# DeltaNet's triangular inverse: levels 1 to 4 on diagonal blocks of 32 rows, and the four chunks written out

## The reference

```python
gamma = jnp.exp(jnp.where(tril, gc[..., :, None] - gc[..., None, :], -jnp.inf))
kb = k * beta[..., None]
low = jnp.where(strict, jnp.einsum('bhncd,bhnsd->bhncs', kb, k) * gamma, 0.0)
rhs = jnp.concatenate([v * beta[..., None], kb * jnp.exp(gc)[..., None]], axis=-1)
sol = lax.linalg.triangular_solve(jnp.eye(c, dtype=low.dtype) + low, rhs,
                                  left_side=True, lower=True)
u, w = sol[..., :dv], sol[..., dv:]
def step(s, xs):
    u_c, w_c, attn_c, qd_c, kd_c, gl_c = xs
    v_new = u_c - jnp.einsum('bhcd,bhde->bhce', w_c, s)
    o = jnp.einsum('bhcd,bhde->bhce', qd_c, s) + jnp.einsum('bhcs,bhse->bhce', attn_c, v_new)
    s = s * jnp.exp(gl_c)[..., None, None] + jnp.einsum('bhcd,bhce->bhde', kd_c, v_new)
    return s, o
```

## Time and profile before

| | us |
|---|---|
| median of 3 runs | 1856.23 |
| lowest and highest | 1850.76, 1856.71 |
| the profiled execution, its own time | 1854.68 |
| span of the profiled execution | 1853.0 |
| one prompt chunk (four of them) | 50.3 to 50.5 |
| the sample chunk, up to its first memory product | 14.4 |

### The profile page before, as it was taken

The page is one execution under the profiler, slowest core; times in us unless marked ns, Lnnn a source line. Parts: engine busy times, 40 slices in busy tenths (PEclk is TensorE's granted clock), DMA queues, the critical chain, the costliest instruction groups (busy, mean ns, idle before and its releaser), DMA issues. The chain is left out here.

```text
span 1853.0 us, 36268 instructions
## 1 busy us (share of the span) xinstructions
PE 1760.0 (95%) x13404; PEld 1636.5 (88%) x13404; DVE 1012.1 (55%) x1848; ACT 722.0 (39%) x1239; POOL 403.2 (22%) x580
## 2 busy tenths in 40 slices
PE   8999899999799999999999999799899999999997
PEld 6999788888598999999999998555598999999997
DVE  4763455551528766767225433576537666678224
ACT  4343333331536333335224311556446333336222
POOL 1554344453001222221000000343300222221000
PEclk9999999998899999999999999899999999999999
DMA  4222211100521222223222224889721222222322
GB/s 174 79 79 80 71 35 35 34 20 1 193 80 57 87 83 79 79 85 102 91 91 69 80 68 156 290 290 326 256 84 54 84 85 79 79 82 75 101 90 86
DMA packets 78367, 188.61 MB, mean 102 GB/s; under 512 B 9442, under 2 KB 25186, under 8 KB 77906
## 3 DMA queue, kind: packets, MB, share of 16 engines
q1 hardware_dynamic: 71618, 168.47, 26.8%
q0 software_dynamic: 6672, 19.10, 3.1%
HBM read 176.00 MB, written 11.55 MB: 101 GB/s over the span
## 5 line engine op out<-in xcount | busy, mean ns | idle before, releaser
L674 PE MATMUL PB<-parts,wparts 128*128 128x288 f32 x8664 | 1170.2, 297 | 21.9 <-DVE wparts L643 10.9
L674 PEld LDWEIGHTS PB<-parts,wparts 128*128 128x128 f32 x8664 | 1164.6, 190 | 26.1 <-DVE wparts L643 21.1
L633 ACT ACTIVATE wparts<-ring 128x1024 fp32r<-128x1024 f32 x198 | 209.8, 1059 | 684.8 <-PE PB L674 683.9
L643 DVE TENSOR_TENSOR wparts<-ring,wparts 128x1024 fp32r<-128x1024 f32 x174 | 212.8, 1224 | 274.3 <-ACT wparts L633 264.7
L1033 POOL COPY cnew<-arena 128x2 f32 (+1 forms) x106 | 115.1, 1085 | 344.0 <-DVE arena L958 341.2
L970 DVE SCALAR_TENSOR_TENSOR arena<-arena,ffw 128x512 f32<-128x512 f32 x176 | 133.7, 760 | 19.4 <-DVE arena L971 12.8
L955 DVE TENSOR_TENSOR arena<-PB,stats 128x288 f32<-128x288 f32 x88 | 40.2, 457 | 127.8 <-PE PB L674 121.2
L684 PE MATMUL PB<-parts,wparts 128*128 128x288 f32 x648 | 104.7, 310 | 3.9 <-DVE parts L513 3.3
L684 PEld LDWEIGHTS PB<-parts,wparts 128*128 128x128 f32 x648 | 91.0, 188 | 12.9 <-DVE parts L513 7.3
L1009 DVE SCALAR_TENSOR_TENSOR arena<-arena,dnw 128x512 f32<-128x512 f32 x54 | 58.0, 1075 | 32.8 <-ACT arena L908 27.6
L932 ACT ACTIVATE arena<-arena,ffw 128x512 f32<-128x512 f32 x88 | 63.8, 725 | 27.0 <-issue 15.5
(11 more groups left out here) (299 smaller groups left out, 2091.8 us busy)
## 6 DMA issues: line engine op xcount, KB each, us to landing
ring<-in_w SPq DMA_DIRECT2D x198, 512.0 KB, 3.2
arena<-in_kpages SPq DMA_DIRECT2D x64, 256.0 KB, 5.5
arena<-in_vpages SPq DMA_DIRECT2D x64, 256.0 KB, 5.2
arena<-in_kpages POOLq DMA_DIRECT2D x64, 128.0 KB, 2.8
arena<-in_vpages POOLq DMA_DIRECT2D x64, 128.0 KB, 5.0
membuf<-in_w SPq DMA_DIRECT2D x8, 512.0 KB, 5.7
arena<-in_state_dn SPq DMA_DIRECT2D x6, 512.0 KB, 5.0
o_dns_s<-arena SPq DMA_DIRECT2D x6, 512.0 KB, 3.9
```

The lines of the kernel that those rows point to most:

```text
L633: nc.scalar.activation(wparts[:, 0, k, :], ring[:, k, :], ACT.Copy).then_inc(hi_ready, 1)
L643: nc.vector.tensor_tensor(wparts[:, 1, k, :], ring[:, k, :], wparts[:, 0, k, :].bitcast(F32), ALU.subtract).then_inc(lo_ready, 1)
L674: last = nc.tensor.matmul(dst(b), wparts[:, part, k, block * P:(block + 1) * P], x[:, row_, b * HALF:(b + 1) * HALF], start=start and part ...
```

## The change

Levels 1 to 4 only join blocks inside the diagonal blocks of 32 rows. The changed kernel keeps for them only those blocks: four blocks of 32 x 32 for a head and chunk, stored as 128 partitions by 32 columns, so that a group of three heads has 96 columns where it had 384. `LTb`, `BTb`, `TXb` (Tm and TT side by side) and `M1b` are these compact tiles. `blocks` issues each product as four products of 32 x 32 x 32: each has its operands on partitions 32i to 32i+31 and writes to PSUM partitions 32i to 32i+31, that is to its own row and column tile of the array. All of a group's results lie in one PSUM bank. One subtraction of 192 columns then serves Tm and TT of a group.

At the start, `lc` forms the compact lower matrix from the four diagonal blocks, `tt0` makes TT in two small steps and Tm by VectorE's own transposition in blocks of 32, so `t0` and its copy on ScalarE fall away. The full `lb` is formed after level 1, and `vt` (the turning of v on TensorE) moves behind level 1 and waits for it. After level 4, `full` spreads the blocks to 128 x 128 (`em` to Tm, `et` to TT, each times the mask `block4`). Levels 5 and 6 are as before, with `kd` behind level 5. GpSimd forms the masks of levels 2 to 4 in one step. The sample chunk, of 64 positions and levels 1 and 2, uses the same steps with two blocks. Finally the loop over chunks is written out, so no register is computed in it.

```diff
-            for step, g in ((kk, 0), (kq, 0), (kk, 1), (kt, 0), (kt, 1), (kq, 1), (vt, 0), (t0, 0), (vt, 1), (t0, 1)):
+            def blocks(out, left, right):
                 for h in range(3):
+                    for i in range(T // 32):
+                        b = slice(32 * i, 32 * i + 32)
+                        last = nc.tensor.matmul(out[b, h, :], left[b, h, :], right[b, h, :], start=True, stop=True)
+                return last
+            for step, g in ((kk, 0), (kq, 0), (kk, 1), (kt, 0), (kt, 1), (kq, 1)):
                 step(g)
             for l in range(1, levels):
+                if l <= 4:
+                    for g in G:
+                        wait("pool", f"bt{min(l, 2)}_{g}")
+                        wait("dve", f"tt0{g}" if l == 1 else f"x{l - 1}_{g}")
+                        blocks(bank_b(2 * g, T), BTb[0:T, g, l - 1, :, :], TXb[g][0:T, 0, :, :]).then_inc(S_, mark(f"m{l}_{g}"))
+                    for g in G:
+                        wait("act", f"m{l}_{g}")
+                        if l == 1:
+                            wait("dve", f"at{g}")
+                        if l < levels - 1:
+                            blocks(bank_b(2 * g + 1, T), TXb[g][0:T, 1, :, :], M1b[g][0:T, 0, :, :])
+                        blocks(bank_b(2 * g + 1, T, 1), M1b[g][0:T, 0, :, :], TXb[g][0:T, 1, :, :]).then_inc(S_, mark(f"x{l}_{g}"))
+                    if l == 1:
+                        vt(0)
+                        vt(1)
+                    continue
...
+            def lc(g):
                 wait("pe", f"bb{g}")
                 wait("dve", f"lt{g}")
+                for i in range(T // 32):
+                    b = slice(32 * i, 32 * i + 32)
+                    last = nc.vector.tensor_tensor(LTb[b, 3 * g:3 * g + 3, :], heads(LT, g, T, T)[b, :, b],
+                                                   bank(4 + g, T, T)[b, :, b], ALU.mult)
+                last.then_inc(S_, mark(f"lc{g}"))
...
-            for step, g in ((kn_, 0), (qn_, 0), (kn_, 1), (lt, 0), (lb, 0), (qn_, 1), (lt, 1), (lb, 1), (tt0, 0), (tt0, 1),
-                            (vb_, 0), (at, 0), (vb_, 1), (at, 1)):
+            for step, g in ((kn_, 0), (qn_, 0), (kn_, 1), (lt, 0), (lc, 0), (qn_, 1), (lt, 1), (lc, 1), (tt0, 0), (tt0, 1),
+                            (at, 0), (at, 1)):
                 step(g)
             for l in range(1, levels):
                 for g in G:
+                    if l <= 4:
...
+                        nc.vector.tensor_tensor(tx, tx, PB[0:T, 2 * g + 1, 96 * x0:192].rearrange("p (x h n) -> p x h n", x=2 - x0, h=3),
+                                                ALU.subtract).then_inc(S_, mark(f"x{l}_{g}"))
+                        continue
...
+                elif l == 1:
+                    lb(0)
+                    lb(1)
+                elif l == 2:
+                    vb_(0)
+                    vb_(1)
+                elif l == 4:
+                    for g in G:
+                        full("em", Tm, 0, g)
+                        full("et", TT, 1, g)
+                elif l == 5:
+                    kd(0)
+                    kd(1)
...
-            with eng.Fori(0, NCH // 2) as i:
+            for i in range(NCH // 2):
```

More of the change, by code:

```diff
@@ L56 @@
 LEVELS_S = 3
+DN_CONST = 8 * P + 6 * 32
 class Steps:
@@ L314, in heads, with heads_b, bank_b @@
             return a[0:rows, 3 * g:3 * g + 3, 0:T]
+        def heads_b(a, g, T=P):
+            return a[0:T, 3 * g:3 * g + 3, :]
+        def bank_b(b, T=P, x=0):
+            return PB[0:T, b, 96 * x:96 * x + 96].rearrange("p (h n) -> p h n", h=3)
         def bank(b, rows=P, T=P):
@@ L341, in dn_table @@
             act += "os0 os1 ol0 ol1 or0 or1"
-            dve = "ga00 ga01 ga02 ga10 ga11 ga12 kn0 qn0 kn1 lt0 lb0 qn1 lt1 lb1 tt00 tt01 vb0 at0 vb1 at1 "
+            dve = "ga00 ga01 ga02 ga10 ga11 ga12 kn0 qn0 kn1 lt0 lc0 qn1 lt1 lc1 tt00 tt01 at0 at1 "
             for l in range(1, n):
                 for g in G:
-                    if l < n - 1:
+                    if l <= 4:
                         dve += f"x{l}_{g} "
-                    dve += f"xt{l}_{g} "
-                if l <= 2:
-                    dve += f"kd{l - 1} wk{l - 1} "
+                    else:
+                        dve += f"x{l}_{g} xt{l}_{g} " if l < n - 1 else f"xt{l}_{g} "
+                if sample:
+                    dve += f"vb{l - 1} kd{l - 1} wk{l - 1} "
+                else:
+                    dve += {1: "lb0 lb1 ", 2: "vb0 vb1 ", 4: "em0 et0 em1 et1 ", 5: "kd0 wk0 kd1 wk1 "}.get(l, "")
+            if sample:
+                dve += "et0 et1 "
             if sample:
@@ L353, in dn_table @@
                 dve += "s0 s1 s2 s3 s4 s5 on0 on1 oz0 oz1"
-            pool = "ug ib vst bt0_0 bt0_1 bt1_0 bt1_1 " + " ".join(f"bt{l}" for l in range(2, n)) + " qd"
+            pool = "ug ib vst bt1_0 bt1_1 bt2_0 bt2_1 " + ("" if sample else "bt5 bt6 ") + "qd"
             if sample:
@@ L1240, in dn_pe @@
                     for h in range(3 * g, 3 * g + 3):
-                        last = nc.tensor.matmul(bank(g, T, T)[:, h - 3 * g, :], BT[0:T, h, 0:T], Tm[0:T, h, 0:T],
+                        last = nc.tensor.matmul(bank(2 * g, T, T)[:, h - 3 * g, :], BT[0:T, h, 0:T], Tm[0:T, h, 0:T],
                                                 start=True, stop=True)
@@ L1256, in dn_pe @@
             for g in G:
-                wait("dve", f"xt{levels - 1}_{g}")
+                wait("dve", f"et{g}" if sample else f"xt{levels - 1}_{g}")
                 wait("dve", f"wk{g}")
@@ new lines, in full @@
+            def full(name, dst, x, g):
+                wait("dve", f"x{4 if not sample else levels - 1}_{g}")
+                n = T // 32
+                nc.vector.tensor_tensor(heads(dst, g, T, T).rearrange("p h (j n) -> p h j n", j=n),
+                                        TXb[g][0:T, x, :, :].unsqueeze(2).to_broadcast([T, 3, n, 32]),
+                                        block4[0:T, 0:T].rearrange("p (j n) -> p j n", j=n).unsqueeze(1).to_broadcast([T, 3, n, 32]),
+                                        ALU.mult).then_inc(S_, mark(f"{name}{g}"))
```

122 lines of the change are left out of this document (73 added, 49 removed).

## The result

The changed kernel takes 1878.75 us (median; 1873.64 to 1881.13) where the kernel before takes 1855.39 in the same comparison: a ratio of 1.012, with an interval of 1.0097 to 1.0144. It is 1.2% slower. The forecast was 1835 us, 1% faster, with a range up to 1863: wrong in its sign, and outside its range.

The account below looks back on a forecast made before the run. TensorE's own work was taken to bound levels 1 to 4. Gains of 1.5 + 7.6 - 1.15 = 7.9 us a chunk, less 2.9 for the clock, leave 5.0, 20 for four chunks: 1835 us, range 1821 to 1863.

Parts of the forecast that it names:

- the written-out loop at zero: Loop over chunks: second chunk (new code) 50.39 us, fourth 50.48, so new code and looping cost nothing.
- the supply is the wall: Small-product levels: instructions come no faster than 15 ns each, 4.4 us a level; 1863 us, chance 0.15.
- the clock: Levels 1 to 5: TensorE's granted clock falls under small tiles and waits, costing 2.9 us a chunk, ends 0 and 4.5.
- The middling supply: Small-product levels: an instruction every 8.5 ns, 2.45 us a level; 1843 us, chance 0.20.
- Level 1: Second chunk up to m2: m1 and m2 start earlier, a gain of 1.5 us a chunk.
- The sample chunk: Sample chunk, two levels: lost turning and copy balance the added lc, et, vb and kd steps; zero within 1 us.
- the line of the columns: VectorE step time by column count, from 384 and 192 columns: 96 columns take 0.17 us, lc's four steps 0.68.
- Tiles that take turns: Small products: four tiles writing one PSUM bank wait for each other, 4.3 us a level; 1863 or 1915 us, chance 0.08.
- the sign that the prediction named against turns: Changed profile: with turns, matmuls of different tiles would start evenly spaced, and not four together.
- the length of the levels where code is kept: Levels 2 to 4: 1.74 us each in place of 4.26 at full clock, 7.6 us saved a chunk.
- the end of the inverse: Levels 5 and 6: return to full size loses 1.15 us a chunk at full clock; kd is covered by level 6.
- the prediction's estimate: TensorE's instruction issue: about 20 cycles at a 1.2 GHz sequencer clock, 16.7 ns each, 4.8 us a level.

Follow-up runs that it names:

- the first run: The kernel before with only its loop over the four chunks written out, old inverse kept: 1857.62 us, ratio 1.0006.
- the third run: The changed kernel with TensorE's code for one chunk in a loop of two rounds inside a loop of two rounds: 1861.31 us, ratio 1.0029.
- the sixth run: The changed kernel with levels 2 to 4 of a prompt chunk as a three-round loop in TensorE's code, chunks written out: 1859.47 us, ratio 1.0022.
- the ninth run: The kernel with levels 2 to 4 looped, chunks written out, plus dense products that nothing reads where TensorE waits: 1858.62 us, ratio 1.0026.
- the eighth run: The kernel with 64-row blocks, plus v's turning moved, em of both groups ahead of et, GpSimd's scaling later: 1838.17 us, ratio 0.9912.
- the seventh run: The changed kernel's scheme with 64-row blocks in levels 1 to 5, masks behind the first waiting for tt0: 1851.16 us, ratio 0.9977.
- the fifth run: The changed kernel with GpSimd's masks of levels 2 to 4 waiting for tt0 of the second group: 1868.0 us, ratio 1.0063.

## Why the prediction was wrong, by its steps

**The step that failed: the written-out loop at zero.** The prediction read from the earlier trace rows that the second chunk, in new code, takes as long as the fourth, and concluded that "neither new code nor looping costs anything at that rate". The rows were read rightly: the first run shows the same. But the rate belongs to the old inverse, 72 instructions in a level of 4.26 us; the change asks for 288 in 1.74, ten times the rate, and this step was not asked again at the new one. In levels 2 to 4 of the second chunk 864 loads and matmuls took 12.98 us, 15.0 ns each; kept code did the same in 8.27 (9.6 ns) at a clock of 0.57. This is 4.7 us a chunk at most, and 2.3 in the fourth (10.6 us). Over the four chunks the three levels took 12.8, 13.0, 12.1 and 10.6 us where 8.2 were forecast: 15.7 of the 38.6 us between the forecast and the profiled execution (1873.64). It is the largest step and not the only one: without it the third and sixth runs stand at 1861 and 1859, still not faster than before, because of the steps below.

**The rival "the supply is the wall"** had the price, 15 ns an instruction, right by accident: it came from a run bound by its columns. Its mechanism was wrong, since kept code is no slower than 6.1 ns (below), so a loop could cure it, and its 1863 us left out what else failed. It was also set up as an alternative to the clock and to the other losses. All came together, and the range's upper end should have been their sum. The middling supply put one rate, 8.5 ns, on all code, where the runs show two, for new code and for kept; and its gain of 5.3 us a chunk would make some 1833.5 us, so the 1840 to 1845 given for it does not lie between its own two sums.

**The clock**: right in kind. It fell in level 1 and came back for good in levels 5 and 6 (0.60, 0.63, 0.70). Its price of 2.9 us a chunk, with ends of 0 and 4.5, fits what the runs show: the ninth run's fourth chunk, at full clock, is 2.3 us shorter than the sixth's, 1.0 us in level 1 and 1.6 in levels 5 and 6, and holds six fillers of 0.22 to 0.49 us in its levels 2 to 4 besides. By an estimate from these rows the price is then some 3.6 us, from 2.3 with fillers that cost nothing to 5.

**Level 1** was to gain 1.5 us up to m2 and lost 1.2 (17.96 us from the chunk's start instead of 16.80). Of the 2.6 us between that and the forecast, m1 came 1.1 later than worked out, 0.8 of it by the two lc: each took 1.08 us to the next step where 0.68 had been read off the line of the columns:

```profile
272.59 1.04 DVE L1467 TENSOR_TENSOR arena<-arena,PB 32x96 f32<-32x96 f32 x4
273.67 0.26 DVE L1478 TENSOR_TENSOR arena<-arena,pconst 128x96 f32<-128x96 f32 x1
```

Then the tt0 of the second group lost 0.8 beside GpSimd, where 0.4 had been added; and the turning of v, with level 2 queued behind it, took 1.51 us at the lower clock, where three products of 0.11 had been counted. The eighth run, with the turning behind level 2 among its four moves, takes 44.5 us for the chunk where the seventh takes 47.1.

**The sample chunk** was put at zero within 1 us, and lost 6.2. What was missed is a cover that was none: the prediction saw the GpSimd steps beside tt0 in the prompt chunks, and did not ask what GpSimd does in the sample chunk at that place. It was the scaling of q (1.00 us) and a piece of the weight scaling (1.89 us). The fifth run gave back 3.8 of the 6.2 us; no run shows what the other 2.4 are.

**Tiles that take turns** (0.08): not so. One group's m in the second chunk, 24 matmuls in four tiles of one bank:

```profile
274.75 0.39 PE L1251 MATMUL PB<-arena 32*32 32x32 f32 x24 [1.86 <-DVE arena L1484]
```

It took 0.39 us, 0.42 with the first load ahead of it, where 0.39 with the load had been worked out. In the trace its matmuls start four together, some 7 ns apart, and a new four starts every 0.03 us; four together is the sign that the prediction named against turns. The Trainium skill (TensorEngine Tiling (Array Packing), Restrictions and Gotchas) has the rule that different row tiles cannot access the same PSUM bank at once. With four diagonal tiles, which write different partitions of the bank, no run here shows a cost of it.

**Nearly right**: the length of the levels where code is kept. Levels 2 to 4, the way back to full size included, take 7.5 us in the third run's chunks 2 and 4 at a clock of 0.84 to 0.85, and 8.27 in its third at 0.57; worked out were 6.1 at full clock (three times 1.74, and 0.87) and 8.2 at half. **Right** is the end of the inverse: levels 5 and 6 take 7.67 us in the third run's third chunk at full clock, against 7.9.

## What to carry to other kernels

Count instructions per microsecond, not only busy time, wherever a change replaces few large products by many small ones, and ask whether the code there is new or kept: a stretch without a gap says only that its own rate was met. A loop helps only if its body is kept, and half as many instructions in larger tiles came out ahead of the smallest tiles here: 46.6 to 47.8 us in the seventh run's first three chunks, 44.4 to 45.2 in the eighth run, against 48.3 to 49.8 with blocks of 32 whose code is kept (the sixth run). That is not tile size alone: the seventh run has the fifth run's wait as well, the eighth its four moves, and blocks of 32 with those were not run; with the clock held by fillers one chunk of 32 took 46.0. Before a step of VectorE with two SBUF operands is put on the critical path, look at what GpSimd does beside it.

## What the runs showed of the hardware

- New code reaches TensorE in 16 KB packets, one for some 254 loads and matmuls. A gap for it was 0.6 to 2.5 us, and in the one looked at closely TensorE was idle for 1.4 us more after its packet had ended (286.4 to 287.85). Over levels 2 to 4 the changed kernel got an instruction every 15.0 ns in the second chunk and every 12.3 in the fourth. A body of one chunk was kept (no packet in three chunks); one of two chunks was fetched anew (14 packets in each round). The Trainium skill (Runtime: NRT & Kernel Launch, Instruction fetch mechanics) has TensorE's instruction memory at 2048 instructions, refilled in blocks of 256, which agrees with both: one chunk's 766 matmuls and as many loads fit, two chunks' do not. It calls the cost of crossing such a block's boundary mostly hidden; here it was not.
- Kept code is issued faster than I had allowed. In the ninth run's fourth chunk this row, with as many loads, makes 192 instructions in 1.18 us, 6.1 ns each:

```profile
381.38 1.18 PE L1257 MATMUL PB<-arena 32*32 32x32 f32 x96
```

- The floor of about 20 cycles an instruction that the Trainium skill has in the same section (Runtime: NRT & Kernel Launch, Instruction fetch mechanics), 16.7 ns by the prediction's estimate, does not hold for that row.
- The granted clock fell to its lower level under 32 x 32 tiles with waits of 1 to 2 us, with or without gaps for code (0.60 and 0.63 in the second chunk of the changed kernel, 0.53 and 0.50 in the sixth run's). Under 64 x 64 tiles it fell as well in the seventh run (0.74 in level 1 of the second chunk, with waits of 2.03, 0.48 and 1.20 us), and it stayed at 1.00 in chunks 2 to 4 of the eighth, which have the first two of these waits and not the third.
